# Loading a trunk kernel's streamed weights in pairs of 2 MB in place of single units of 1 MB

## What is computed

```python
for l in range(2):
    mod = silu(c) @ w_mod[l] + b_mod[l]
    sh_mix, sc_mix, gt_mix, sh_ffn, sc_ffn, gt_ffn = split(mod, 6)
    h = rms_norm(x, g_mix_pre[l]) * (1 + sc_mix) + sh_mix
    proj = h @ w_in[l]                       # 1024 x 5120: q,k,v of two branches, two gates
    y = sigmoid(g_a) * (stick_breaking(q,k,v) @ w_proj_sb[l]) \
      + sigmoid(g_b) * (block_attention(q,k,v, rel_bias) @ w_proj_moba[l])
    x = x + gt_mix * rms_norm(y @ w_out[l], g_mix_post[l])
    h = rms_norm(x, g_ffn_pre[l]) * (1 + sc_ffn) + sh_ffn
    if l == 0: y = (silu(h @ w1) * (h @ w3)) @ w2              # dense, inner width 3584
    else:      y = sum over 8 experts of combine[e] * swiglu(h, w1[e], w3[e], w2[e])
                                                              # top 2 of 8 by a router
    x = x + gt_ffn * rms_norm(y, g_ffn_post[l])
```

## Time and profile before

| what | value |
|---|---|
| time, median of 3 runs | 1674.56 us (1674.24 to 1675.97) |
| time of the profiled execution | 1675.27 us |
| span in its profile | 1673.4 us |
| mean granted TensorE clock | 0.991 |
| TensorE matmul busy | 1625.0 us, 97% |
| VectorE busy | 1397.6 us, 84% |
| ScalarE busy | 1122.2 us, 67% |
| HBM read | 511.88 MB |

### The profile page before, as it was taken

How to read it: one execution, slowest core, us unless ns; L and a number is a source line. 1 busy time by engine, 2 the same in 40 slices (tenths; PEclk the granted TensorE clock), 3 DMA queues, 4 the chain that set the end, 5 groups by cost and what they waited for, 6 DMA issues and landing times.

```text
span 1673.4 us, 23549 instructions
## 1 busy us (share of the span) xinstructions
PE 1625.0 (97%) x7850; PEld 1339.6 (80%) x7850; DVE 1397.6 (84%) x1691; ACT 1122.2 (67%) x1389; POOL 108.1 (6%) x209
## 2 busy tenths in 40 slices
PE   8999989999989998899999999999999999999996
PEld 6977768888879776788888888888888888888885
DVE  7977777787687567798988989989989989989987
ACT  4665454344455564578878878778778778778784
POOL 0120010000011101620000000000000000000000
PEclk9999999999999999899999999999999999999999
DMA  9955547777568344599999999999999999999993
GB/s 386 390 233 217 186 154 298 279 267 283 201 238 361 132 150 150 204 373 361 355 377 364 365 374 361 359 376 359 366 367 363 374 363 363 368 369 378 350 368 121
DMA packets 74014, 514.85 MB, mean 308 GB/s; under 512 B 9108, under 2 KB 10333, under 8 KB 12254
## 3 DMA queue, kind: packets, MB, share of 16 engines
q1 hardware_dynamic: 72226, 508.64, 79.8%
q0 software_dynamic: 1152, 4.19, 0.7%
q10 hardware_dynamic: 572, 1.18, 0.2%
HBM read 511.88 MB, written 2.11 MB: 307 GB/s over the span
## 4 chain that ended last, share of the span: by engine, by line
PE 88%; DVE 4%; ACT 3%; issue 3%; POOL 1%; DMA 0%; DVEq 0%; ACTq 0%; POOLq 0%
PE ps L1426 27%; PE ps L1428 26%; PE ps L1427 26%; PE ps L1708 2%; DVE wlo L318 1%; ACT whi L310 1%; DVE raw L327 1%; ACT vals L711 1%; PE ps L1570 1%; DVE qk L1027 1%; PE ps L1590 0%; PE ps L1448 0%; PE ps L1903 0%; PE ps L1876 0%; PE ps L1904 0%
## 5 line engine op out<-in xcount | busy, mean ns | idle before, releaser
L318 DVE TENSOR_TENSOR wlo<-raw,whi 128x1024 fp32r<-128x1024 f32 x868 | 1015.9, 1221 | 148.0 <-ACT whi L310 147.7
L310 ACT ACTIVATE whi<-raw 128x1024 fp32r<-128x1024 f32 x868 | 867.6, 1053 | 211.1 <-PE ps L1428 208.5
L1426 PE MATMUL ps<-whi,hhi 128*128 128x512 f32 x1568 | 624.5, 398 | 11.1 <-DVE hlo L839 5.0
L1428 PE MATMUL ps<-wlo,hhi 128*128 128x512 f32 x1568 | 612.8, 391 | 0.0
L1427 PE MATMUL ps<-whi,hlo 128*128 128x512 f32 x1568 | 612.6, 391 | 0.0
L1426 PEld LDWEIGHTS ps<-whi,hhi 128*128 128x128 f32 x1568 | 295.2, 188 | 78.0 <-issue 8.7
L1428 PEld LDWEIGHTS ps<-wlo,hhi 128*128 128x128 f32 x1568 | 295.0, 188 | 63.1
L1427 PEld LDWEIGHTS ps<-whi,hlo 128*128 128x128 f32 x1568 | 295.5, 188 | 59.2 <-issue 1.1
L1426 PE MATMUL ps<-whi,ohi 128*128 128x512 f32 x432 | 173.5, 402 | 2.3 <-issue 2.3
L1428 PE MATMUL ps<-wlo,ohi 128*128 128x512 f32 x432 | 169.2, 392 | 0.0
L1427 PE MATMUL ps<-whi,olo 128*128 128x512 f32 x432 | 168.6, 390 | 0.0
(11 more groups left out here) (222 smaller groups left out, 1091.8 us busy)
## 6 DMA issues: line engine op xcount, KB each, us to landing
raw<-in_w_moe SPq DMA_DIRECT2D x336, 1024.0 KB, 6.9
raw<-in_w_pre_moe SPq DMA_DIRECT2D x98, 1024.0 KB, 4.9
raw<-in_w_mod_units SPq DMA_DIRECT2D x48, 1024.0 KB, 5.3
x<-in_x SPq DMA_DIRECT2D x2, 512.0 KB, 4.8
bias<-dist_scratch SPq DMA_DIRECT2D x1, 1024.0 KB, 9.7
xn_rows<-wide ACTq DMA_DIRECT2D x2, 512.0 KB, 4.5
out<-x SPq DMA_DIRECT2D x1, 512.0 KB, 2.6
out<-x SPq DMA_DIRECT2D x2, 256.0 KB, 2.1
```

Source lines behind the costliest of these rows:

```text
L310: nc.scalar.activation(whi[:, s % SPLIT, part], raw[:, slot(s), part], ACT.Copy).then_inc(hi_done, 1)
L318: nc.vector.tensor_tensor(wlo[:, s % SPLIT, part], raw[:, slot(s), part], whi[:, s % SPLIT, part].bitcast(F32), ALU.subtract).then_inc(lo_ ...
L1426: nc.tensor.matmul(out, a_hi, b_hi, start=first, stop=False, **kw)
L1428: return nc.tensor.matmul(out, a_hi, b_lo, start=False, stop=last, **kw)
```

## The change

Two neighbours of the ring become one load. The host lays out two consecutive positions (or two consecutive expert units) side by side, so that each partition holds both in one run of 16 KB, and the load writes two neighbouring slots of `raw`. Three semaphores `pair_full`, one for each pair of slots, replace the six `raw_full`. SyncE waits until both units that lay in the two slots are done with, then issues one load of 2 MB. A consumer of either half waits for the whole pair. The small write and the bias load keep their place behind the loads of the pairs at positions 6 and 10. The order in which units are consumed, the number of slots and all work on the other engines stay as they are.

```diff
-        raw_full = [sem(f"raw_full{i}") for i in range(RAW)]
+        pair_full = [sem(f"pair_full{i}") for i in range(RAW // 2)]
...
-                act.wait_ge(raw_full[slot(s)], dma_value(s, r))
+                act.wait_ge(pair_full[slot(s) // 2], dma_value(s, r))
...
-            dve.wait_ge(raw_full[pos % RAW], 16 * (pos // RAW + 1))
+            dve.wait_ge(pair_full[pos % RAW // 2], 16 * (pos // RAW + 1))
...
             def load(s, r, src):
-                sp.wait_ge(lo_done, number(s, r) * 2 - (2 * RAW - 2))
-                sp.dma_start(raw[:, slot(s), :], src).then_inc(raw_full[slot(s)], 16)
+                sp.wait_ge(lo_done, number(s + 1, r) * 2 - (2 * RAW - 2))
+                first = slot(s)
+                sp.dma_start(raw[:, first:first + 2, :], src.rearrange("p (u n) -> p u n", u=2))\
+                    .then_inc(pair_full[first // 2], 16)
...
-            for pos, (kind, n) in enumerate(RING):
+            for pos in range(0, len(RING), 2):
                 if pos >= RAW:
-                    was, m = RING[pos - RAW]
-                    if was == "unit":
-                        sp.wait_ge(lo_done, 2 * m + 2)
-                    else:
-                        sp.wait_ge(mod_done, 2 * m + 2)
-                src = pre_units[n] if kind == "unit" else mod_units[n]
-                sp.dma_start(raw[:, pos % RAW, :], src).then_inc(raw_full[pos % RAW], 16)
-                if pos == 7:
+                    for was, m in RING[pos - RAW:pos - RAW + 2]:
+                        if was == "unit":
+                            sp.wait_ge(lo_done, 2 * m + 2)
+                        else:
+                            sp.wait_ge(mod_done, 2 * m + 2)
+                first = pos % RAW
+                sp.dma_start(raw[:, first:first + 2, :], ring_pairs[pos // 2].rearrange("p (u n) -> p u n", u=2))\
+                    .then_inc(pair_full[first // 2], 16)
+                if pos == 6:
...
-                if pos == 11:
+                if pos == 10:
...
-                    for j in range(6):
-                        load(BLOCK0 + 6 + j, item * FBLK + b, moe_units[e * FFN_UNITS + b * 6 + (4 + j)])
+                    for j in range(0, 6, 2):
+                        load(BLOCK0 + 6 + j, item * FBLK + b, moe_pairs[e * (FFN_UNITS // 2) + b * 3 + (2 + j // 2)])
...
+    ring = [mods[n] if kind == "mod" else pre[n] for kind, n in RING]
+    out["w_ring"] = np.stack([np.concatenate(ring[i:i + 2], axis=1) for i in range(0, len(ring), 2)])
...
+    out["w_moe"] = moe.reshape(-1, 2, P, UNIT).transpose(0, 2, 1, 3).reshape(-1, P, 2 * UNIT)
```

More of the change, by code:

```diff
@@ L90, with build @@
         MODS_AFTER[max(n for kind, n in RING[:_pos] if kind == "unit")].append(_n)
-def build(nc, x_d, c_d, mod_units, b_mod, g_rows, pre_units,
-          rel_bias, w_router, moe_units, onehot_d, dist_scratch, xn_rows, out_d):
+def build(nc, x_d, c_d, b_mod, g_rows, ring_pairs,
+          rel_bias, w_router, moe_pairs, onehot_d, dist_scratch, xn_rows, out_d):
     with ExitStack() as ctx:
@@ L398, in load_later_blocks @@
                 with sp.Fori(0, FBLK - 1) as b:
-                    for j in range(6):
-                        load(BLOCK0 + 6 + j, item * FBLK + b, moe_units[e * FFN_UNITS + b * 6 + (4 + j)])
+                    for j in range(0, 6, 2):
+                        load(BLOCK0 + 6 + j, item * FBLK + b, moe_pairs[e * (FFN_UNITS // 2) + b * 3 + (2 + j // 2)])
             def load_down(item, prev, first):
-                for j in range(2):
-                    load(BLOCK0 + first + j, item * FBLK, moe_units[prev * FFN_UNITS + (FFN_UNITS - 2 + j)])
+                load(BLOCK0 + first, item * FBLK, moe_pairs[prev * (FFN_UNITS // 2) + (FFN_UNITS // 2 - 1)])
             def load_item(item, e, prev):
-                for j in range(4):
-                    load(BLOCK0 + j, item * FBLK, moe_units[e * FFN_UNITS + j])
+                for j in range(0, 4, 2):
+                    load(BLOCK0 + j, item * FBLK, moe_pairs[e * (FFN_UNITS // 2) + j // 2])
                 load_down(item, prev, 4)
                 load_later_blocks(item, e)
-            for j in range(4):
-                load(MOE0 + j, 0, moe_units[j])
+            for j in range(0, 4, 2):
+                load(MOE0 + j, 0, moe_pairs[j // 2])
             load_later_blocks(0, 0)
@@ L2035, in _layout @@
     moe = np.concatenate([_ffn_units(*(inputs[k][0, e] for k in ("w1_moe", "w3_moe", "w2_moe"))) for e in range(E)])
-    out = {"x": inputs["x"], "c": inputs["c"], "w_mod_units": mods}
+    pre = np.concatenate([mixers[0], dense, mixers[1]])
+    ring = [mods[n] if kind == "mod" else pre[n] for kind, n in RING]
+    out = {"x": inputs["x"], "c": inputs["c"]}
     out["b_mod"] = inputs["b_mod"]
@@ L2039, in _layout @@
                                                                      "g_ffn_post")])
-    out["w_pre_moe"] = np.concatenate([mixers[0], dense, mixers[1]])
+    out["w_ring"] = np.stack([np.concatenate(ring[i:i + 2], axis=1) for i in range(0, len(ring), 2)])
     out.update({k: inputs[k] for k in ("rel_bias", "w_router")})
-    out["w_moe"] = moe
+    out["w_moe"] = moe.reshape(-1, 2, P, UNIT).transpose(0, 2, 1, 3).reshape(-1, P, 2 * UNIT)
     return out
```

## The result

The changed kernel takes 1679.08 us (median of 6 runs, 1678.12 to 1682.66), the kernel before, run beside it, 1674.47 us (6 runs, 1674.24 to 1675.97). The ratio is 1.0032, with a 95% interval of 1.0020 to 1.0043: the change costs 4.6 us, more than the 0.2% that can be told from nothing. The profiled execution took 1678.82 us with a span of 1677.0 us, at a mean granted clock of 0.991, the same as before.

A forecast was written before the change was run, and what follows sets the result against it. TensorE was taken to set the pace from 60 us on, VectorE before. Only the start's +0.3 us counted: 1675.27 became 1675.6, forecast as 1674.9 since the profiled execution lay 0.7 above the median; range 1671.5 to 1681, its own 1672.5 to 1677.5.

The forecast's parts named there:

- the start and the mixers pay: Rival: pairs landing in 9.5 to 10.5 us delay start and mixers, 4 to 6 us, 1679 to 1681; chance 0.06.
- The price of a load: Issue to landing of a 2 MB pair: 7.2 us at the start, 7.2 to 9.5 in the experts, at worst 11.4.
- (1) SyncE's issues: On SyncE, 241 loads issued in place of 482; the engine does nothing else, so no gain.
- (2) The start: VectorE's first modulation unit comes 0.87 us later, at 12.1, as half of a pair; +0.3 us, bounds 0 and 0.87.
- (3) The first 60 us: Unit 6's pair, behind the bias load, lands 0.3 us before its split; cost 0, bounds 0 and 1 us once.
- (4) From 60 to 76 us: Unit 10's pair 1.3 us late, but TensorE has some 3.5 us to spare; cost 0, second mixer the same.
- (5) The experts: Tightest place has 9.1 us; a 9.5 us pair is 0.4 late, within TensorE's lead of 3.2 us; cost 0.
- The shallow ring: Rival, in the experts: landings over 10.9 us slow the ring's turn; at 11.5, 31 us, 1705; chance 0.09.
- The faster rival: The DMA side was the limit: at most 2.3 us gained, 1672.3, with the clock 1670.5; chance over 0.2%: 0.05.

The follow-up runs named there:

- late but not whole: Against the kernel before: two 1 MB loads issued back to back once both slots are free, a semaphore for each slot; 1674.44 us, ratio 1.0000.
- the threes: Against the kernel before: the experts' 1 MB loads issued when three slots are free, usable when all three have landed; 1812.31 us, ratio 1.0826.
- the layout alone: The kernel before, with its 482 single loads and six semaphores, reading from the paired layout in HBM; 1674.94 us, ratio 1.0000.

## Why the prediction was right in its range and wrong in its steps

The forecast was 1674.9, within 1672.5 to 1677.5, with 80% for no measurable change; slower had 0.15. The time, 1679.08, lies outside that and a measurable 4.6 us up. It is inside the wide range of 1671.5 to 1681 only since the high end was set by the rival that had 0.06 ("the start and the mixers pay", 1679 to 1681). So the range held by its rival, not by its account. By its steps:

**The price of a load** was too low. I took 7.2 us for a pair alone; it is 8.3, and never under 7.9. For the experts 7.2 to 9.5, near the lower end; it is 9.7 in the median and up to 12.1, above even the 11.4 that I had called the worst. The rate is not what failed: the first three pairs, issued together, landed at 11.4, 16.3 and 21.2, which is 2.45 us for 1 MB. What failed is the sum of the fixed 2.2 us and twice the 2.48: two loads of 1 MB need 7.6 from the first issue to the second landing, one load of 2 MB 7.8 with rows of 8 KB and 8.3 with rows of 16 KB. Why, no run here tells. And the 8.3 is the price far from other loads: the pairs issued from 17 to 75 us took 8.6 to 11.2. The trace of before could have told that, since its single loads issued from 43 to 58 us took 5.2 to 7.8 and not 4.7. The Trainium skill's fit (DMA: Bandwidth & Descriptors, "Anatomy of one DMA"), which is for the GpSimd path, gives an estimated 6.8 us; the trace's 8.3 is further from it than from my 7.2, and the measurement decides.

**(1) SyncE's issues**: right, 241 loads, nothing gained.

**(2) The start**, +0.3 us: right within what one execution can tell. VectorE's first modulation unit began at 11.47, not at 12.1, and 1.32 us of waiting for its load show; a round later it stood at 17.80, 0.4 ahead of before, in the second trace at 18.69, 0.5 behind.

**(3) The first 60 us**, 0: right in the cost, not in the reason. The bias landed after 11.9 us in place of 9.7, and the pair behind it took 10.8 and landed at 47.4. Its split was to have 0.3 us to spare and waited 1.47:

```profile
47.36 2.01 ACT L310 ACTIVATE whi<-raw 128x1024 fp32r<-128x1024 f32 x2 [1.47 <-DMA raw<-in_w_ring]
```

None of this reached TensorE: VectorE's remainders of units 6 and 7 were 0.40 us ahead of before, as at the start. The lateness was absorbed, which I had not counted on.

**(4) From 60 to 76 us**, 0: this is the step that failed. I priced the pair of unit 10 alone, at 1.3 us late. The 1.59 us of idle before its split look like that, but by luck: the pair was issued at 61.0 and took 10.4 us, not 7.2, and the split began at 71.41, 4.2 us later than before; the rest of that lateness had already come with the split ahead. For I did not price the pair of unit 9, whose free slots at 54.9 leave 6.5 us, less than 7.2 and far less than the 9.3 it took. And I asked only when TensorE needs the unit, over 5.8 us later, not what else stands behind the split on ScalarE. That part of the step held: in the run that is late but not whole the split of unit 10 waited 1.4 us and nothing was lost. I had written that what stands behind it is late too, and then checked it against one user only. Behind unit 9 stood the copies out of PSUM, and TensorE wanted their banks at once: 1.42 us of waiting, 1.65 us in all. The run with the copies moved shows that it waited for them. For the second mixer the forecast of 0 was right: waits of up to 4.0 us stand there between 493 and 515 us, and TensorE is as busy as before. From 460 to 530 us, the kernel before, then the changed one (columns as in the earlier trace rows):

```profile
460.00:530.00 70.00, 64.44 (x431) 57.61 (x430) 56.73 (x78) 38.55 (x51) 6.32 (x13) 1.00 0.77 307
```

```profile
460.00:530.00 70.00, 64.39 (x431) 57.59 (x430) 56.80 (x78) 38.76 (x50) 8.33 (x13) 1.00 0.77 306
```

**(5) The experts**, 0: wrong by 2.6 to 2.8 us. The price of the pair is the reason that the rows show; that the wait is again for something behind the split is shown at two places, one in each trace, and for the rest of the loss it is argued. The tightest place had 9.1 us; the forecast pair of 9.5 would have been 0.4 late, a real one of 12 is 3 late, as much as the lead of 3.2 that I gave it. And that lead is TensorE's on the weights; the copies of the inner activations behind the split have none of it (L730, then `olo`, then TensorE's 1.15 us). TensorE never waits for `wlo`, as I expected; an item is 121.7 us where all goes well.

**The rivals.** The shallow ring had its threshold at a landing of 10.9 us. Six of 154 landings pass it, the median doesn't, so the ring catches up and the loss stays at 2.6 us in place of 31; that the model of the turn is right, the threes show. The rival that came true got its chance from a landing of 9.5 to 10.5; I held it at 0.06 since I trusted 7.2. Its sum of 4 to 6 us fits, but partly by luck: of its parts only the mixer's 1 to 3 us came, the first turns of the ring and the bias cost nothing, and the 2.6 us of the experts were not in it. The faster rival fell: in the experts the stream is no faster than before, as the 361 GB/s show, so batching beyond 1 MB found nothing to gain where loads already overlap.

## What to carry to other kernels

Joining neighbouring slots of a ring into one load spends slack twice, once because the load is asked for later and once because its first half is usable later; either alone may be free where both are not, so sum both against the shortest time from free slot to first use. Whether a deeper ring would give the slack back, no run here tests. Price a larger load by a measured one, in the stretch where it will run, not by the rate of a full queue. When an instruction that works in order will be late, go through everything behind it on its engine and ask who wants that, not only who wants its own result.

## What the runs showed that I had not expected

**Small transfers on other queues slow down.** The page gives the median from issue to landing of the gather of an expert's tokens, on GpSimd's queue: first of the kernel before, then of the changed one.

```profile
qk<-xn_rows,idx POOLq DMA_INDIRECT x8, 8.2
```

```profile
qk<-xn_rows,idx POOLq DMA_INDIRECT x8, 11.8
```

It is 9.8 to 10.1 us in the three kernels that issue late and in pairs but move rows of 8 KB, 11.0 to 12.2 with pairs of 16 KB rows in the experts, and 7.9 to 8.6 where the experts' loads are single. So part comes with the issue in pairs and part with the long rows. The second part would fit the rule of the Trainium skill (DMA: Bandwidth & Descriptors, "Queues, rings and completion order") that a DMA engine changes queues only between packets; no run here tests the rule itself. The write of the normalised rows takes 8.3 us in place of 4.5, and 8.5 to 8.7 with the rows of 8 KB issued in pairs, so the length of the rows is not what slows it. Neither is on the path here.

**The granted clock wanders between executions of one kernel.** Stretches of 3.4 us at 1.2 GHz come and go. From 141 us on, the kernel before, then the changed one (columns as in the earlier trace rows, the clock is the third number from the end); TensorE is busy all the time in both:

```profile
141.00:144.30 3.30, 3.30 (x9) 2.54 (x8) 2.80 (x12) 2.55 (x9) 0.00 (x0) 0.50 0.63 268
```

```profile
141.00:144.30 3.30, 3.30 (x20) 2.72 (x17) 2.51 (x10) 1.13 (x5) 0.00 (x0) 1.00 0.91 293
```

The kernel with the layout alone has no such stretch at 141 us but one at 469, the second trace of the changed kernel has both, and near 663 us the stretch at 1.2 GHz is 17.1 us long in eleven of the thirteen traces and 20.5 in two, the changed kernel's first and that with pairs ahead of the experts alone. The one at 141 us costs 1.7, the longer one near 663, where TensorE also stands idle twice, for 5.5 and 2.6 us, costs 1.2 more than the shorter. This is a large part of the 3 to 5 us by which single executions of one kernel differ, and a reason to read the loss from places in two traces and not from two spans.
